# Three more convolution taps on VectorE, later waits ahead of the down products, and ten side tiles per feed-forward block moved to its down chunks

## The chip, the cores and the metric

The kernel runs on one core of a Trainium2 chip. The metric is the device time of one execution in microseconds (us), as the median over runs. The kernel writes its instructions for each engine by hand: TensorE (PE) multiplies, VectorE (DVE) adds and scales, ScalarE (ACT) applies activations and copies, GpSimd (POOL) and SyncE (SP) mostly issue transfers (DMA).

## The reference

Four layers in two blocks work on 256 tokens of width 1024, in float32 (the first layer also has 256 context tokens). Each layer is: half a feed-forward block (FFN), a mixer, another half FFN. A modulation vector per layer, the product of a 1024-wide condition with a 1024 x 9216 matrix, shifts, scales and gates each of them.

```python
def swiglu(y, w_gu, w_down):
    gate, up = jnp.split(y @ w_gu, 2, axis=-1)          # 1024 -> 2 x 2816
    return (jax.nn.silu(gate) * up) @ w_down            # 2816 -> 1024

def half_ffn(h, m, off, g, w_gu, w_down):
    y = modulate(h, g, m[off], m[off + 1])
    return h + 0.5 * m[off + 2] * swiglu(y, w_gu, w_down)

def odd_mixer(y, w_in, conv_w, conv_b, cnorm_g, pool_w, pool_scale, w_out):
    z = y @ w_in
    ga, gb, q = jnp.split(z, [D_CONV, 2 * D_CONV], axis=-1)      # D_CONV = 768
    u = ga * jax.nn.sigmoid(gb)
    u = conv_general_dilated(u, conv_w, ...) + conv_b            # depthwise, 31 taps
    u = jax.nn.silu(rmsnorm(u, cnorm_g))
    ...
    return jnp.concatenate([u, p], axis=-1) @ w_out
```

The other mixers (a recurrent one, a gated linear attention, a latent attention) are not touched.

## The kernel before

**The eight FFNs.** They are F[0] to F[7] in the order of their run. F[0] works on 512 tokens (`wide_one`), the others on 256. Each runs 15 chunks: 11 gate chunks (`u` = 0 to 10, each 256 of the 2816 gate columns and the same of the up columns, 2 MB of weights), then 4 down chunks (`d` = 0 to 3, each 256 of the 1024 outputs, 2.8 MB of weights). A chunk is a matrix product of 2 x 2 blocks done in seven products after Strassen and Winograd. Product `p` takes a sum of weight blocks and a sum of token blocks (table `PRODUCT`) and goes to a PSUM bank pair (BX, BY, BQ, BZ, BW). PE does them in the order 1, 4, 2, 6, 7, 5, 3. In a gate chunk a product is 8 matmuls, in a down chunk 11, one for each "unit tile" `k` of 256 hidden columns, which gate chunk `k` made. The trace has two records for one of these float32 matmuls.

**What DVE does beside it.** The weight sums S1 (L2739), S2 (L2744), S3 (L2748) and S4 (L2753); the sums of token blocks of each unit tile, T1, T2, T4 and T3 (L2762 to L2769, called by `hidden_sums`); and the additions that read the products. In a down chunk these are: the addition of BX to X (L2860), then the sum that empties BY (L2870), then S4, the sum with BZ (L2875), and more. Product 5 writes to BY, so it waits until L2870 has read product 6. The last thing on DVE in a chunk but one is S1 of the next chunk, which waits for that chunk's weights.

**The waits at the first down chunk.** T4 of the last unit tile is made after the last gate chunk's last product has been read, activated and multiplied (L2826, L2827, an activation on ACT, L2830, then T1, T2, T4). Product 4 reads T4 of all 11 unit tiles, and waits for the last of them ahead of its first matmul.

**Weights.** SP loads them into two slots (W0, W1) in turn. The load for a chunk is issued when the chunk two before it has ended (`free`), as two transfers. So the weights of down chunk `d` travel while chunk `d`-1 runs.

**Row tiles.** The modulation vectors of layers 0 to 3 are mostly made on DVE: a row tile (128 x 1024 of the matrix, 512 KB) is multiplied by the condition and summed along its rows in one instruction (L2692, function `ada`). 36 tiles are done in each of F[1] to F[6], none in F[7]. The list `some` says how many per chunk. Tiles lie in a ring of 8 buffers (ADAW). POOL issues the load of a tile as soon as the tile 8 before it has been used (L2406), so a tile used is at once a tile loaded. In a gate chunk the tiles come after S3; in a down chunk all but one come after S3, ahead of the addition of BX to X, and the last one after L2860's third call.

**The convolution** is in layer 1, between F[2] and F[3]. Its 768 channels are 6 stages `f` of 128. Of its 31 taps the first `VTAPS` are done on DVE, as one multiply-add (L1454) each over 128 x 256, two stages side by side; the other `PTAPS` are matmuls on PE with a diagonal matrix that ACT makes (L1407, L1389). When both are done, DVE adds the two parts (L1460), and the squares, their sum on PE and the norm follow.

```python
for f in range(CT_):                    # PE
    pe.wait_ge(s_dg, f + 1)
    pe.wait_ge(s_cu, f + 1)
    for k in range(PTAPS):
        last = mm(PS[CBANK[f]][:, 0:S], DIAG[:, f % 3, k], UP[:, f, VTAPS + k:VTAPS + k + S], ...)
```

Of the kernel before, what the change touches and what calls it, by code (L numbers as in the profile page):

```python
# [19 lines left out]
PAIRS = FT // 2  # L20
# [148 lines left out]
def build(nc, t, out, table_at, stop=None):  # L169

    stop = STOP if stop is None else stop
    with ExitStack() as ctx:
# [200 lines left out]
        def block_bank(b, q, half):  # L373
            at = half * q if b[0] == b[1] else 0
            return PS[b[q]][:, at:at + half]
# [21 lines left out]
        s_th = sem("hidden_sums_ready")  # L397
        s_wh = sem("wide_hidden_sums_ready")
        s_fa = sem("small_ffn_scalar_step")
        s_fd = sem("small_ffn_vector_step")  # L400
# [927 lines left out]
        QM = region(6016, [2, S])  # L1328
        POOLM = region(6528, [4, 2, S])
        SQC = region(8704, [CT_, S])  # L1330
        VTAPS = 20
        PAD = CW // 2
        CBANK = (0, 1, 2, 3, 4, 6)
        PTAPS = CW - VTAPS
        DIAG = region(10240, [3, PTAPS, P])
# [859 lines left out]

        mixers = {}

        some = [0] + [2] * 10 + [4] * 4
        F = [block_ffn(f1[0], d1[0], [2, 4, 4, 4, 4, 4, 5, 7, 7, 7, 8] + [0] * 4, 0, 2, 0.5, 2 * S)]
        mixers["rwkv"] = rwkv_plan()  # L2200
        F += [block_ffn(f2[0], d2[0], some, 0, 8, 0.5),
# [225 lines left out]
        def _(pe):  # L2427
# [11 lines left out]
            def ffn(sec, n_y):  # L2439
                t0, td, n0, fa0, fd0, i = [sec[name] for name in ("t0", "td", "n0", "fa0", "fd0", "i")]  # L2440
                wide_one = sec["T"] > S
# [54 lines left out]
                def down_waits(d, p):  # L2496
                    n_ = n0 + PAIRS + d
                    fa, fd = fa0 + 3 * PAIRS + d, fd0 + 5 * PAIRS + 6 * d
                    if p == 1:
                        pe.wait_ge(s_fd, fd - 5 if d else fd - 2)  # L2500
                    elif p == 2:
                        pe.wait_ge(s_fa, fa + 1)
                    elif p == 3:
                        pe.wait_ge(s_s4, n_ + 1)
                        pe.wait_ge(s_ev, td + 7 * d)
                    elif p == 4:
                        if d:
                            pe.wait_ge(s_fd, fd - 2)
                        elif wide_one:
                            pe.wait_ge(s_wh, 3)  # L2510
                        else:
                            pe.wait_ge(s_th, 4 * PAIRS * i - 1)
                    elif p == 5:
                        pe.wait_ge(s_fd, fd + 2)
                    elif p == 6:
                        pe.wait_ge(s_s2, n_ + 1)
                        pe.wait_ge(s_fd, fd - 1)
                    elif p == 7:
                        pe.wait_ge(s_s3, n_ + 1)
                        if d:  # L2520
                            pe.wait_ge(s_fd, fd)
                        elif wide_one:
                            pe.wait_ge(s_wh, 4)
                        else:
                            pe.wait_ge(s_th, 4 * PAIRS * i)

                for d in range(4):
                    c = sec["w0"] + PAIRS + d
                    w = down_blocks(sec, PAIRS + d)
                    pe.wait_ge(s_w[c % 2], 32 * (c // 2 + 1))  # L2530
                    for p in order_of(sec, PAIRS + d):
                        left, right, b = PRODUCT[p]
                        down_waits(d, p)
                        for k in range(PAIRS):
                            last = mm(block_bank(b, 0, half), w[left][:, k], hb[right][:, k],  # L2535
                                      start=(k == 0 and p not in (2, 5)), stop=(k == PAIRS - 1),
                                      skip_group_check=p in (2, 5))
                        last.then_inc(s_mm, 1)
# [486 lines left out]
```

## Time and profile before

| | |
|---|---|
| median of 3 runs | 3040.9 us (3039.69 to 3043.85) |
| the profiled execution's own time | 3042.03 us |
| its span in the trace | 3040.2 us |
| PE busy | 2874.1 us (95%) |
| DVE busy | 2041.0 us (67%) |
| DMA engines, mean rate | 169 GB/s |

The span runs from the first to the last instruction of the profile, and the execution's own time is 1.8 us more. Times in the timelines count from the start of the span. A release in brackets behind a row, "[1.26 <-DVE ARENA L2768]", says how long the engine sat idle before this row, and what ended it.

### The profile page before, as it was taken

The page shows a single profiled execution, that of the slowest core. Times are in us where ns is not written, and L with a number is a line of the kernel's source. Part 1 is how long each engine was busy: PE and PEld are TensorE (multiplying, and loading weights), DVE is VectorE, ACT ScalarE, POOL GpSimd, SP SyncE. Part 2 cuts the span into 40 slices and gives each one's busy share as a digit, 9 for nine tenths or more (in the row PEclk, how much of TensorE's full clock was granted, in tenths as well). Part 3 has the DMA queues.
Part 4 walks back from the last instruction along what each step waited for, and adds up shares of the span by engine and source line. Part 5 has one row for each costly group of instructions (what it writes and reads, how often), then busy time and mean ns, then how long its engine had stood idle before and what let it go on. Part 6 is the DMA issues. An engine that isn't in the chain of part 4 may idle for free.

```text
span 3040.2 us, 62638 instructions
## 1 busy us (share of the span) xinstructions
PE 2874.1 (95%) x27464; PEld 2658.5 (87%) x27464; DVE 2041.0 (67%) x3534; ACT 568.9 (19%) x1283; POOL 306.4 (10%) x518
## 2 busy tenths in 40 slices
PE   7999998889888999999999999989999999998998
PEld 6888886777887999998889999977889989977998
DVE  6777537545664887885668878826258878853664
ACT  2000004343332101002210021024111021032101
POOL 0001002422430000000000100000000100000000
PEclk8999999999999999999999999999999999999999
DMA  7557313013005686786257867643367857823452
GB/s 277 166 184 244 109 45 108 4 45 98 18 4 181 213 272 222 243 265 213 70 191 253 284 199 255 219 119 111 127 213 254 283 177 251 263 73 97 139 187 91
DMA packets 387503, 514.53 MB, mean 169 GB/s; under 512 B 14032, under 2 KB 344976, under 8 KB 386080
## 3 DMA queue, kind: packets, MB, share of 16 engines
q1 hardware_dynamic: 347632, 366.73, 37.3%
q0 software_dynamic: 39456, 143.67, 13.8%
q8 instruction: 217, 3.56, 0.5%
q14 instruction: 54, 0.44, 0.0%
q10 hardware_dynamic: 144, 0.13, 0.0%
HBM read 509.44 MB, written 1.05 MB: 168 GB/s over the span
## 4 chain that ended last, share of the span: by engine, by line
PE 86%; DVE 5%; DMA 4%; ACT 3%; issue 2%; POOL 1%; SPq 0%; DVEq 0%; ACTq 0%; POOLq 0%
PE PS L2491 39%; PE PS L2535 19%; PE PS L630 6%; PE PS L650 5%; PE PS L807 3%; PE PS L1706 2%; PE PS L2547 2%; PE PS L1631 2%; DMA W<-in_ffn_out 1%; DMA W<-in_ffn_w_down 1%; PE PS L1389 1%; PE PS L2435 1%; PE PS L1483 1%; PE PS L2568 1%; PE PS L666 1%
## 5 line engine op out<-in xcount | busy, mean ns | idle before, releaser
L2491 PE MATMUL PS<-Y,W 128*128 128x128 f32 (+1 forms) x5456 | 713.2, 289 | 36.3 <-ACT Y L2628 30.5
L2491 PEld LDWEIGHTS PS<-Y,W 128*128 128x128 f32 x5456 | 677.9, 195 | 55.4 <-issue 35.0
L2491 PE MATMUL PS<-Y,ARENA 128*128 128x128 f32 (+1 forms) x3872 | 477.7, 280 | 0.0
L2491 PEld LDWEIGHTS PS<-Y,ARENA 128*128 128x128 f32 x3872 | 458.5, 192 | 4.5
L2535 PE MATMUL PS<-ARENA,W 128*128 128x128 f32 (+1 forms) x2816 | 364.2, 288 | 10.8 <-DVE ARENA L2768 7.9
L2535 PEld LDWEIGHTS PS<-ARENA,W 128*128 128x128 f32 x2816 | 346.9, 192 | 22.3 <-DVE ARENA L2768 9.7
L2406 POOL DMA_DIRECT2D ADAW<-in_ada_rows x272 | 144.4, 532 | 1873.1 <-DVE ADAW L2692 1527.7
L2692 DVE SCALAR_TENSOR_TENSOR ADAW<-ADAW,CB 128x1024 f32<-128x1024 f32 x280 | 332.0, 1219 | 0.2
L2739 DVE TENSOR_TENSOR ARENA<-W 128x1024 f32<-128x1024 f32 (+1 forms) x120 | 159.3, 1327 | 12.9 <-DMA W<-in_ffn_out 4.9
L2748 DVE TENSOR_TENSOR W<-W 128x1024 f32<-128x1024 f32 (+1 forms) x120 | 158.9, 1324 | 0.0
L2744 DVE TENSOR_TENSOR ARENA<-ARENA,W 128x1024 f32<-128x1024 f32 (+1 forms) x116 | 152.5, 1314 | 0.3
L2535 PE MATMUL PS<-ARENA 128*128 128x128 f32 x1232 | 146.7, 275 | 0.0
L630 PE MATMUL PS<-Y,W 128*128 128x256 f32 (+2 forms) x560 | 128.0, 392 | 15.0 <-ACT Y L2628 13.1
L2535 PEld LDWEIGHTS PS<-ARENA 128*128 128x128 f32 x1232 | 142.1, 192 | 0.0
L650 PE MATMUL PS<-W 64*64 64x64 f32 x4608 | 114.2, 223 | 27.3 <-issue 24.0
L630 PEld LDWEIGHTS PS<-Y,W 128*128 128x128 f32 (+2 forms) x560 | 107.7, 193 | 35.2 <-issue 14.9
L2600 ACT ACTIVATE SIL<-SIL 128x256 f32<-128x256 f32 x77 | 32.1, 417 | 565.5 <-DVE SIL L2826 565.5
L650 PEld LDWEIGHTS PS<-W 64*64 64x64 f32 x4608 | 100.3, 136 | 38.9 <-issue 35.0
L807 PE MATMUL PS<-Y,W 128*128 128x256 f32 x528 | 123.6, 394 | 10.7 <-ACT Y L2628 4.6
L807 PEld LDWEIGHTS PS<-Y,W 128*128 128x128 f32 x528 | 102.5, 197 | 31.5 <-issue 13.4
L2753 DVE TENSOR_TENSOR ARENA<-W,ARENA 128x1024 f32<-128x1024 f32 x88 | 107.2, 1218 | 0.0
L1317 DVE SCALAR_TENSOR_TENSOR X<-PS,HG,X 128x256 f32<-128x256 f32 x32 | 15.5, 484 | 125.0 <-PE PS L630 50.9
(425 smaller groups left out, 3736.3 us busy)
## 6 DMA issues: line engine op xcount, KB each, us to landing
ADAW<-in_ada_rows POOLq DMA_DIRECT2D x272, 512.0 KB, 4.7
W<-in_ffn_w_gu SPq DMA_DIRECT2D x88, 1024.0 KB, 7.6
W<-in_ffn_in SPq DMA_DIRECT2D x88, 1024.0 KB, 7.4
W<-in_ffn_w_down SPq DMA_DIRECT2D x32, 1408.0 KB, 9.3
W<-in_ffn_out SPq DMA_DIRECT2D x32, 1408.0 KB, 9.2
W<-in_even_w_in SPq DMA_DIRECT2D x40, 512.0 KB, 4.6
W<-in_e_w_in SPq DMA_DIRECT2D x16, 512.0 KB, 4.9
W<-in_e_w_in SPq DMA_DIRECT2D x8, 1024.0 KB, 7.5
```

Of the source, the lines that this page charges most:

```text
L630: last = mm(PS[idx % 4][0:m_, 0:S], wide(c, kt, n_)[:, k, q * P:q * P + m_], x(k), start=(k == 0), stop=(k == kt - 1))
L650: last = mm(to, x, y, start=(k == 0), stop=(k == len(pairs) - 1))
L807: last_ = mm(PS[at[f] % 4][:, 0:S], w[:, k, q * P:(q + 1) * P], Y[:, k, off:off + S], start=(k == 0), stop=(k == DT - 1))
L1631: last = mm(PS[idx % 4][:, 0:S], wide(c, DT)[:, k, (i % 2) * P:(i % 2 + 1) * P], Y[:, k, 0:S], start=(k == 0), stop=(k == DT - 1))
L2406: pool.dma_start(ADAW[:, g % 2, i], t["ada_rows"][g * P:(g + 1) * P, i * D:(i + 1) * D])\
L2491: last = mm(block_bank(b, q, half), w[left][:, k, q * P:(q + 1) * P], yb[right][:, k], start=(k == 0 and p not in (2, 5)), stop=(k == 3), ...
L2535: last = mm(block_bank(b, 0, half), w[left][:, k], hb[right][:, k], start=(k == 0 and p not in (2, 5)), stop=(k == PAIRS - 1), skip_group_ ...
L2692: V.scalar_tensor_tensor(w, w, 1.0, CB[:, 0 if layer < 2 else 1], ALU.mult, ALU.mult, accum_out=MOD[:, layer, tile + i:tile + i + 1]).then ...
L2739: V.tensor_tensor(w["S1"], w["A21"], w["A22"], ALU.add).then_inc(s_s1, 1)
L2744: V.tensor_tensor(w["S2"], w["S1"], w["A11"], ALU.subtract).then_inc(s_s2, 1)
L2748: V.tensor_tensor(w["S3"], w["A11"], w["A21"], ALU.subtract).then_inc(s_s3, 1)
L2753: V.tensor_tensor(w["S4"], w["A12"], w["S2"], ALU.subtract).then_inc(s_s4, 1)
```

## The change

It does three things. `VTAPS` goes from 20 to 23, so `PTAPS` from 11 to 8. The list `some` goes from 2 row tiles in each of the gate chunks 1 to 10 and 4 in each down chunk to 1 in each gate chunk and 6, 6, 7, 7 in the down chunks; the sum stays 36. And in down chunk 0 of F[1] to F[7], PE waits ahead of products 1 and 4 only for what unit tile 9 and the banks need, and for unit tile 10 ahead of the last matmul of the product.

```diff
-        VTAPS = 20
+        VTAPS = 23
...
-        some = [0] + [2] * 10 + [4] * 4
+        some = [0] + [1] * 10 + [6, 6, 7, 7]
...
                     if p == 1:
-                        pe.wait_ge(s_fd, fd - 5 if d else fd - 2)
+                        if d:
+                            pe.wait_ge(s_fd, fd - 5)
+                        else:
+                            pe.wait_ge(s_fa, fa - 1)
+                            pe.wait_ge(s_fd, fd - 7)
...
                         elif wide_one:
                             pe.wait_ge(s_wh, 3)
                         else:
-                            pe.wait_ge(s_th, 4 * PAIRS * i - 1)
+                            pe.wait_ge(s_fd, fd - 2)
+                            pe.wait_ge(s_th, 4 * (PAIRS * i - 1))
...
                         for k in range(PAIRS):
+                            if d == 0 and k == PAIRS - 1:
+                                if p == 1:
+                                    pe.wait_ge(s_fd, fd0 + 5 * PAIRS - 2)
+                                elif p == 4 and not wide_one:
+                                    pe.wait_ge(s_th, 4 * PAIRS * i - 1)
                             last = mm(block_bank(b, 0, half), w[left][:, k], hb[right][:, k], ...)
```

The lines after the first added one move down: PE's matmul of the down chunks is L2535 before and L2545 after, and DVE's lines from L2692 on are 10 higher.

PE at the start of down chunk 0 of F[1], products 1, 4 and 2, before (hidden_sums_ready counts T1 to T4, small_ffn_vector_step counts DVE's additions and multiplications):

```order
L2535 MATMUL PS<-ARENA,W 128x128 [waits small_ffn_vector_step,weights_loaded1]
L2535 MATMUL PS<-ARENA,W 128x128 x10
L2535 MATMUL PS<-ARENA,W 128x128 [waits hidden_sums_ready]
L2535 MATMUL PS<-ARENA,W 128x128 x10
L2535 MATMUL PS<-ARENA,W 128x128 [waits small_ffn_scalar_step]
```

The same place after the change:

```order
L2545 MATMUL PS<-ARENA,W 128x128 [waits small_ffn_vector_step,small_ffn_scalar_step,weights_loaded1]
L2545 MATMUL PS<-ARENA,W 128x128 x9
L2545 MATMUL PS<-ARENA,W 128x128 [waits small_ffn_vector_step]
L2545 MATMUL PS<-ARENA,W 128x128 [waits hidden_sums_ready,small_ffn_vector_step]
L2545 MATMUL PS<-ARENA,W 128x128 x9
L2545 MATMUL PS<-ARENA,W 128x128 [waits hidden_sums_ready]
L2545 MATMUL PS<-ARENA,W 128x128 [waits small_ffn_scalar_step]
```

Each of the two products has a wait of its own ahead of its eleventh matmul now.

DVE in down chunk 1 of F[1], from S3 to S4, before (modulation_rows_loaded0 to 7 are the buffers of the ring):

```order
L2748 TENSOR_TENSOR W<-W 128x11x128
L2692 SCALAR_TENSOR_TENSOR ADAW,MOD<-ADAW,CB 128x1024 [waits modulation_rows_loaded0]
L2692 SCALAR_TENSOR_TENSOR ADAW,MOD<-ADAW,CB 128x1024 [waits modulation_rows_loaded1]
L2692 SCALAR_TENSOR_TENSOR ADAW,MOD<-ADAW,CB 128x1024 [waits modulation_rows_loaded2]
L2860 SCALAR_TENSOR_TENSOR X<-PS,HG,X 128x128 [waits dense_tile_done]
L2870 TENSOR_TENSOR SIL<-JUNK,PS 128x128 [waits dense_tile_done,small_ffn_scalar_step]
L2753 TENSOR_TENSOR X<-W,ARENA 128x1408 [waits weight_sum2_ready]
```

After the change:

```order
L2758 TENSOR_TENSOR W<-W 128x11x128
L2702 SCALAR_TENSOR_TENSOR ADAW,MOD<-ADAW,CB 128x1024 [waits modulation_rows_loaded0]
L2702 SCALAR_TENSOR_TENSOR ADAW,MOD<-ADAW,CB 128x1024 [waits modulation_rows_loaded1]
L2702 SCALAR_TENSOR_TENSOR ADAW,MOD<-ADAW,CB 128x1024 [waits modulation_rows_loaded2]
L2702 SCALAR_TENSOR_TENSOR ADAW,MOD<-ADAW,CB 128x1024 [waits modulation_rows_loaded3]
L2702 SCALAR_TENSOR_TENSOR ADAW,MOD<-ADAW,CB 128x1024 [waits modulation_rows_loaded4]
L2870 SCALAR_TENSOR_TENSOR X<-PS,HG,X 128x128 [waits dense_tile_done]
L2880 TENSOR_TENSOR SIL<-JUNK,PS 128x128 [waits dense_tile_done,small_ffn_scalar_step]
L2763 TENSOR_TENSOR X<-W,ARENA 128x1408 [waits weight_sum2_ready]
```

Five tiles instead of three stand ahead of the addition of BX and the sum that empties BY (L2880 now).

## Rows read from the trace of the kernel before

**Rows 1.** The page: span, PE and DVE busy (us, share, instructions)

```profile
span 3040.2 us, 62638 instructions
PE 2874.1 (95%) x27464; PEld 2658.5 (87%) x27464; DVE 2041.0 (67%) x3534; ACT 568.9 (19%) x1283; POOL 306.4 (10%) x518
```

**Rows 2.** Timeline of PE in the convolution (start, length)

```profile
1474.78 5.02 PE L1389 MATMUL PS<-ARENA 128*128 128x256 f32 x22
1479.72 2.00 PE L1397 MATMUL PS<-ARENA 128*64 128x256 f32 x16
1481.65 24.02 PE L1389 MATMUL PS<-ARENA 128*128 128x256 f32 x110
```

**Rows 3.** Timeline of DVE in the convolution

```profile
1473.30 15.13 DVE L1454 SCALAR_TENSOR_TENSOR ARENA<-ARENA,VEC 128x256 f32<-128x256 f32 x38
1488.53 0.75 DVE L1460 TENSOR_TENSOR ARENA<-ARENA,PS 128x256 f32<-128x256 f32 x2
...
1505.71 0.42 DVE L1460 TENSOR_TENSOR ARENA<-ARENA,PS 128x256 f32<-128x256 f32 x1 [4.33 <-PE PS L1389]
```

**Rows 4.** Groups by line and shape: busy, mean ns, idle before, its releasers

```profile
L2535 PE MATMUL PS<-ARENA,W 128*128 128x128 f32 x2464 | 286.4, 275 | 8.7 <-DVE ARENA L2768 6.3 <-DMA W<-in_ffn_out 1.8 <-DMA W<-in_ffn_w_down 0.5
L2739 DVE TENSOR_TENSOR ARENA<-W 128x1408 f32<-128x1408 f32 x32 | 52.0, 1625 | 9.5 <-DMA W<-in_ffn_out 4.9 <-DMA W<-in_ffn_w_down 3.9
```

**Rows 5.** Timeline of PE, start of down chunk 0 of F[2]

```profile
1343.83 2.62 PE L2535 MATMUL PS<-ARENA,W 128*128 128x128 f32 x22
1347.71 5.18 PE L2535 MATMUL PS<-ARENA,W 128*128 128x128 f32 x44 [1.26 <-DVE ARENA L2768]
```

**Rows 6.** Timeline of DVE, same place

```profile
1343.37 1.62 DVE L2739 TENSOR_TENSOR ARENA<-W 128x1408 f32<-128x1408 f32 x1 [0.70 <-DMA W<-in_ffn_w_down]
...
1347.37 0.29 DVE L2768 TENSOR_TENSOR ARENA<-ARENA 128x128 f32<-128x128 f32 x1
...
1350.85 1.22 DVE L2692 SCALAR_TENSOR_TENSOR ADAW<-ADAW,CB 128x1024 f32<-128x1024 f32 x1
...
1354.29 0.34 DVE L2860 SCALAR_TENSOR_TENSOR X<-PS,HG,X 128x128 f32<-128x128 f32 x1
1355.46 0.29 DVE L2870 TENSOR_TENSOR SIL<-JUNK,PS 128x128 f32<-128x128 f32 x1 [0.83 <-PE PS L2535]
```

**Rows 7.** Timeline of PE, start of down chunk 0 of F[6]

```profile
2609.06 2.72 PE L2535 MATMUL PS<-ARENA,W 128*128 128x128 f32 x22 [1.76 <-DMA W<-in_ffn_out]
2613.39 5.18 PE L2535 MATMUL PS<-ARENA,W 128*128 128x128 f32 x44 [1.61 <-DVE ARENA L2768]
```

**Rows 8.** Windows, down chunks 1 and 2 of F[2], then of F[7] (PE, PEld, DVE, ACT, POOL, clock, DMA share, GB/s)

```profile
1362.60:1379.80 17.20, 17.20 (x157) 17.20 (x156) 13.86 (x23) 0.28 (x1) 2.12 (x4) 1.00 0.87 291
1379.80:1397.00 17.20, 17.20 (x157) 17.20 (x156) 13.71 (x23) 0.28 (x1) 2.12 (x4) 1.00 0.87 291
2970.00:2987.20 17.20, 17.20 (x156) 17.20 (x155) 9.38 (x15) 0.28 (x1) 0.00 (x0) 1.00 0.52 170
2987.20:3004.40 17.20, 17.20 (x156) 17.20 (x155) 9.37 (x15) 0.28 (x1) 0.00 (x0) 1.00 0.53 169
```

**Rows 9.** Timeline of PE, starts of down chunks 2 and 3 of F[2]

```profile
1379.75 7.53 PE L2535 MATMUL PS<-ARENA,W 128*128 128x128 f32 x66
...
1396.95 3.29 PE L2535 MATMUL PS<-ARENA,W 128*128 128x128 f32 x28
```

**Rows 10.** Timeline of DVE in down chunks 1 and 2 of F[2]

```profile
1372.65 0.29 DVE L2870 TENSOR_TENSOR SIL<-JUNK,PS 128x128 f32<-128x128 f32 x1 [2.17 <-PE PS L2535]
...
1378.94 1.62 DVE L2739 TENSOR_TENSOR ARENA<-W 128x1408 f32<-128x1408 f32 x1
...
1396.37 1.62 DVE L2739 TENSOR_TENSOR ARENA<-W 128x1408 f32<-128x1408 f32 x1 [0.35 <-DMA W<-in_ffn_w_down]
```

**Rows 11.** Weight load of down chunk 3 by its line: issue, landing; F[2]

```profile
L2359 SPq DMA_DIRECT2D W<-in_ffn_w_down x2: 368/751/1134, 1379.9 to 1380.4; - x2
...
DMA to landing us min/median/max: 8.6/12.3/15.9
```

**Rows 12.** The same load in F[7]

```profile
DMA to landing us min/median/max: 6.3/8.1/9.9
```

## The prediction

> **What bounds the kernel now.** I read the page's first part, then the groups with what ended their idle time, then timelines of PE and DVE at the three places that the change touches, and last the windows and the landing times of the weight loads. PE is busy 2874.1 of 3040.2 us [rows 1], so only what shortens PE's work or removes a wait of PE counts. DVE has a third of the span free, but not everywhere: in a down chunk it is busy 13.86 of 17.20 us [rows 8].
>
> Three places matter. (1) In the convolution PE does its products back to back and DVE waits 4.33 us for each of the last ones [rows 2, 3]. (2) At the step from gate to down chunks of F[1] to F[7], PE's idle time is 8.7 us in all: 6.3 for T4 (L2768) and 2.3 for late weights [rows 4]. (3) In the down chunks PE doesn't wait, but the weights come just in time: in F[2] S1 of chunk 3 waited 0.35 us for them, 0.58 us ahead of the chunk's own start [rows 9, 10].
>
> **Term 1, the taps.** The last five stages of 11 products take 24.02 us [rows 2]; the steps are 4.75 us (DVE's 4.33 of idle and 0.42 of work, [rows 3]), so one product takes 0.432. 3 x 6 = 18 go: 7.8 us. DVE gets 18 more multiply-adds of 15.13/38 = 0.398 us [rows 3], 7.2 us: its taps end at 1488.53 + 7.2 = 1495.7 instead of 1488.5, and after five additions of 0.75/2 it would be at 1497.6. PE ends at 1505.7 - 7.8 = 1497.9 and releases the sixth and last. So DVE's work is covered by PE's with nearly nothing to spare, and the gain is the full 7.8. If a tap cost DVE the full 0.48 of a lone one (no row hints at it), 1.2 us of it would go. I take -7.8. ACT makes 18 diagonals less, which nothing waits for: PE's products run on without a gap there.
>
> **Term 2, the wait for T4.** Product 1 of down chunk 0 starts at 1343.83 in F[2]; a product of 11 matmuls takes 17.20/7 = 2.46 us [rows 9]. Product 4 could start at 1346.29 and starts at 1347.71 [rows 5]. With the wait at the eleventh matmul, T4 is needed 10 x 2.46/11 = 2.2 us later. No wait of F[1] to F[7] exceeds 1.61 [rows 7] where 2.2 are given, so all 6.3 us go there. The same change at product 1 gives nothing: PE waited there for weights alone [rows 4].
>
> But they come back at product 5, which waits for L2870. From the start of T4 (1347.37) to the start of L2870 without its wait are 1355.46 - 0.83 - 1347.37 = 7.3 us [rows 6]; two more row tiles of (1354.29 - 1350.85)/3 = 1.15 each make it 9.6. It would end at 1357.2. PE, no longer stopped, is at product 5 at 1343.83 + 5 x 2.46 = 1356.1. So it stops there for 1.1 us, and of 1.26 only 0.16 is kept. What can help is that T4 itself comes earlier: S1 of the first down chunk waits 0.70 us for its weights, and DVE holds T4 up behind it [rows 6]. The move takes one row tile's load out of the last gate chunks. I price a tile from the windows: (0.87 - 0.52) x 17.20/4 = 1.5 us of all DMA engines [rows 8]. That covers the 0.70 and, in F[6] and F[1], most of the 2.3 us by which PE waited for weights [rows 4, 7]. Bounds: between 0.5 (only F[7], which has no row tiles) and 8.7. I take the middle, -4.4.
>
> **Term 3, ten more tiles in the down chunks.** DVE has the time: it has 3.3 us free in a chunk [rows 8]; two tiles need 2.3, three need 3.4. Of its idle time 2.17 us stand right before L2870 [rows 10], where most of the tiles go, so there it is just used up. I put 0.2 us for each of 12 chunks with more tiles than fit well at a third of them: +0.8.
>
> The transfers are the other half. Each tile used is a tile loaded. With four tiles a chunk the DMA engines are busy 0.87 of the time, without any 0.52 [rows 8]; at 1.5 us a tile, six make 0.87 + 3.0/17.2 = 1.04, and seven 1.13. The weights of the next chunk are in that queue. Their second transfer lands 15.9 us after its issue at 1380.4 with four tiles [rows 11], and 9.9 us after without [rows 12]: again 1.5 us for a tile. PE needs them at 1396.95, S1 at 1396.02, and they land at 1396.3 [rows 9 to 11]: 0.7 us of margin. The upper bound is the whole delay: two tiles, 3.0 us, less 0.9 of margin at chunk 2 (S1 there ran at 1378.94 and PE at 1379.75), and three tiles, 4.5 less 0.7 at chunk 3, less the 2.1 by which the chunk is late already: 3.8 for an FFN, 23 for six. The lower bound is nothing. What speaks for less than the bound: in chunk 1 the tiles come some 1.1 us later against the weights, since DVE is later; the tiles at the end of a burst may land in the next chunk; and all 32 S1 of this size waited 8.8 us for weights [rows 4], 0.3 on average, so other FFNs have more margin than F[2]. I take a third: +7.
>
> **The sum.** -7.8 - 4.4 + 7.8 = -4.4 us on the profiled execution, which took 3042.0 us, 1.1 above the median. On the median: 3040.9 - 4.4 = 3036.5; I say 3036.
>
> The Trainium skill (DMA: Bandwidth & Descriptors, section "Queues, rings and completion order") says that each DMA engine goes round the queue rows that have work and drains a whole packet of descriptors from one before it turns to the next. By that rule a row tile that is queued is not held back by the weights, so each of them delays their last bytes as long as any are left. The 1.5 us for each of four tiles agrees with it [rows 11, 12]. By the rule term 3 would be at its upper bound, which is the second rival.
>
> **The rivals.** *Hidden loads:* the additional tiles travel in the time that the DMA engines have left, and the weights are not later. For it: a share of 0.87 leaves 2.2 us, and the longer bursts may end in the next chunk's start, where the weights are only issued. Against it: 1.04 and 1.13 are more than there is. Then term 3 is 0 to 1, and the sum -12: 3029. *Late weights in full:* the row tiles' bursts are served before the last of the weights, at 1.5 us each. Term 3 is then +23.8, the sum +11.6: 3053. It is one mechanism, and decides as soon as the weights of chunks 2 and 3 come late by 11.4/6 = 1.9 us for an FFN: there the gain of terms 1 and 2 is gone. *Taps only, the rest a draw:* delays of 8 to 16 us eat term 2 and most of term 1, sum -4 to +4 around 3041; it differs from my forecast in size alone. *The waits do nothing:* PE stops at product 5 for as long as it did at product 4. That is inside term 2's bound.
>
> **How the numbers follow.** A measurement here tells changes of over 0.2%, 6.1 us, from none. Forecast (sum -9 to 0): 0.45, of which 0.14 lie beyond -6.1. Hidden loads (-10 to -16): 0.26. The draw (0 to +6): 0.15. Late weights in full (over +6): 0.14. So faster 0.40, same 0.46, slower 0.14. The forecast's own range is 3032 to 3041. The range for 8 in 10 takes most of the hidden loads and of the late weights: 3027 to 3049.
>
> **What would show it.** In the convolution: L1389 with x16 records for a stage, 3.45 us apart, and the last L1460 at 7.8 us less from the first; if it waits for no PE, DVE has become the bound. At down chunk 0: no idle time of PE for L2768 (L2778 now); idle time of about 1 us ahead of product 5 for L2880 would show the stall moved. In the down chunks: DMA share near 1.0 where it was 0.87, and idle time of PE ahead of chunks 2 and 3 for W. No such idle time is the first rival, over 2 us for an FFN the second. The prediction is most likely wrong in term 3, which I could only bound.

## The result, and the profile after

The changed kernel took 3053.25 us in the median of 5 runs (3051.6 to 3063.3); the kernel before took 3041.34 in the median of its 5. The ratio is 1.0043, with a 95% interval of 1.0024 to 1.0062: slower by 0.4% (the ratio is estimated from all the runs and is not the quotient of the two medians, 1.0039). The prediction was 3036, with a range of 3027 to 3049: the time lies outside the range, and the change went the other way. The time measured is that of the second rival, late weights in full (3053).

The profiled execution took 3053.18 us. Its page: span and busy times, and the shares of the engines in the chain that ended last. Before, DMA had 4% of that chain and PE 86%.

```profile
span 3051.4 us, 62573 instructions
PE 2872.0 (94%) x27428; PEld 2657.4 (87%) x27428; DVE 2043.1 (67%) x3552; ACT 563.2 (18%) x1265; POOL 306.6 (10%) x518
PE 81%; DMA 7%; DVE 5%; ACT 3%; issue 2%; POOL 1%; SPq 0%; DVEq 0%; ACTq 0%; POOLq 0%
```

PE has 18 products of the convolution less, 7.8 us, and yet it is busy only 2.1 us less than in [rows 1]. The groups by line and shape say why:

```profile
L2545 PE MATMUL PS<-ARENA,W 128*128 128x128 f32 x2464 | 294.6, 281 | 18.6 <-DMA W<-in_ffn_w_down 9.8 <-DMA W<-in_ffn_out 8.7
L2545 PE MATMUL PS<-ARENA 128*128 128x128 f32 x1232 | 147.2, 275 | 1.9 <-DVE SIL L2880 1.9
L2749 DVE TENSOR_TENSOR ARENA<-W 128x1408 f32<-128x1408 f32 x32 | 52.0, 1624 | 29.5 <-DMA W<-in_ffn_w_down 15.2 <-DMA W<-in_ffn_out 13.6
```

Against [rows 4]: the T4 wait (6.3 us) is gone from the first row, and 18.5 us of waits for weights stand in its place, where there were 2.3. The same 2464 records take 294.6 us instead of 286.4. DVE's S1 (L2749 now) waits 28.8 us for weights instead of 8.8.

**Where PE waits** for weights is one place in each of F[1] to F[6]: ahead of down chunk 2 (0.5 us more come at chunk 0 of F[1]). Timeline of PE in F[2], from down chunk 0 to 2:

```profile
1347.00 7.53 PE L2545 MATMUL PS<-ARENA,W 128*128 128x128 f32 x66
...
1359.93 2.72 PE L2545 MATMUL PS<-ARENA 128*128 128x128 f32 x22 [0.48 <-DVE SIL L2880]
...
1364.94 7.53 PE L2545 MATMUL PS<-ARENA,W 128*128 128x128 f32 x66
...
1384.36 9.26 PE L2545 MATMUL PS<-ARENA,W 128*128 128x128 f32 x66 [2.05 <-DMA W<-in_ffn_w_down]
```

The first row answers to [rows 5]: products 1, 4 and 2 now run without a stop. The second is the stall at product 5 that the prediction had worked out; it is 0.48 us where 1.1 were expected. The last row is the loss. PE waits 2.05 us for weights, and then the same three products take 9.26 us instead of 7.53. Windows of F[2] show what the second part is: the idle stretch, the start of chunk 2 and its rest (columns as in [rows 8]).

```profile
1382.20:1384.30 2.10, 0.10 (x1) 0.00 (x0) 0.00 (x0) 0.00 (x0) 0.00 (x0) 1.00 0.71 268
1384.40:1387.40 3.00, 3.00 (x16) 3.00 (x17) 3.00 (x3) 0.00 (x0) 0.00 (x0) 0.58 0.98 326
1388.50:1403.20 14.70, 14.70 (x134) 14.70 (x134) 13.93 (x26) 0.28 (x1) 3.71 (x7) 1.00 0.96 324
```

After the wait the granted clock is 0.58 for 3 us, so mostly the lower of its two levels, 1.2 GHz, and PE does 16 records in them; from 1388.5 on it is 1.00, 2.4 GHz, with 27 records in 3 us (134 in 14.7). From the starts of chunks 2 and 3 in the timelines, chunk 2 takes 18.9 us in F[1] to F[6] (18.7 in F[5]) instead of 17.2. That is 10.1 us in all, in slower records and not in waits. The first row of the groups agrees, if it is set against the version without any such wait further down (294.6 - 284.5 = 10.1); before, that row had 286.4 us, 1.9 more than a version without T4's waits.

**The weights.** The load of down chunk 2 in F[2] by its line:

```profile
L2359 SPq DMA_DIRECT2D W<-in_ffn_w_down x2: 367/944/1522, 1365.1 to 1365.5; - x2
...
DMA to landing us min/median/max: 8.8/13.8/18.8
```

Before, this load took 15.7 us; now 18.8, and 20.9 in F[1] instead of 16.1. Chunk 3's, on which the prediction counted for nearly half of its bound, delays nothing. In F[2] it is issued by 1382.7, when chunk 1 has ended, and lands 14.5 us later, at 1397.2; chunk 3 starts at 1403.3, because chunk 2 itself started late and ran 1.7 us longer.

**The convolution** went as predicted. PE, then DVE:

```profile
1480.25 3.72 PE L1389 MATMUL PS<-ARENA 128*128 128x256 f32 x16
...
1485.83 17.54 PE L1389 MATMUL PS<-ARENA 128*128 128x256 f32 x80
```

```profile
1501.13 1.75 DVE L1460 TENSOR_TENSOR ARENA<-ARENA,PS 128x256 f32<-128x256 f32 x5
1503.41 0.42 DVE L1460 TENSOR_TENSOR ARENA<-ARENA,PS 128x256 f32<-128x256 f32 x1 [0.54 <-PE PS L1389]
```

PE's last five stages take 17.54 us instead of 24.02, and the first takes 3.72 instead of 5.02: 7.8 less. DVE still waits for PE at the last addition, 0.54 us, where the prediction had 0.3.

**The ledger.** The stretches between the starts of chunks, as PE's timeline has them, after minus before, summed over the FFNs:

| stretch | us |
|---|---|
| from the end of F[2] to F[3], with the convolution | -8.6 |
| from the last gate chunk to down chunk 1, F[1] to F[7] | -7.3 |
| down chunk 1 with the wait behind it, F[1] to F[6] | +19.1 |
| down chunk 2, F[1] to F[6] | +10.1 |
| all else (the head alone -3.4) | -2.2 |
| sum | +11.1 |

Stretches that the change does not touch differ by up to 6 us between two executions (the one between F[0] and F[1] was 0.4 longer here, 6.2 longer in rows_only below), so below only the stretches that a question is about are compared.

### The profile page after: what moved, and what is told of

The parts are those of the page before. It is cut to its first block, busy times and chain, and to the rows that moved or that the text cites. A ratio compares the mean times of both kernels' runs of the same rounds, so it can differ in the third digit from the quotient of the medians.

```text
span 3051.4 us, 62573 instructions
## 1 busy us (share of the span) xinstructions
PE 2872.0 (94%) x27428; PEld 2657.4 (87%) x27428; DVE 2043.1 (67%) x3552; ACT 563.2 (18%) x1265; POOL 306.6 (10%) x518
## 4 chain that ended last, share of the span: by engine, by line
PE 81%; DMA 7%; DVE 5%; ACT 3%; issue 2%; POOL 1%; SPq 0%; DVEq 0%; ACTq 0%; POOLq 0%
PE PS L2491 39%; PE PS L2545 15%; PE PS L630 6%; PE PS L650 5%; PE PS L807 3%; DMA W<-in_ffn_w_down 3%; DMA W<-in_ffn_out 3%; PE PS L1706 2%; PE PS L2557 2%; PE PS L1631 2%; PE PS L2435 1%; PE PS L1483 1%; DVE ADAW L2702 1%; PE PS L1389 1%; PE PS L2578 1%
## 5 line engine op out<-in xcount | busy, mean ns | idle before, releaser
L2545 PE MATMUL PS<-ARENA,W 128*128 128x128 f32 (+1 forms) x2816 | 372.4, 293 | 20.6 <-DMA W<-in_ffn_w_down 9.8
L2545 PEld LDWEIGHTS PS<-ARENA,W 128*128 128x128 f32 x2816 | 355.9, 196 | 31.7 <-DMA W<-in_ffn_w_down 10.6
L2749 DVE TENSOR_TENSOR ARENA<-W 128x1024 f32<-128x1024 f32 (+1 forms) x120 | 159.3, 1328 | 33.1 <-DMA W<-in_ffn_w_down 15.2
L2545 PE MATMUL PS<-ARENA 128*128 128x128 f32 x1232 | 147.2, 275 | 1.9 <-DVE SIL L2880 1.9
L2545 PEld LDWEIGHTS PS<-ARENA 128*128 128x128 f32 x1232 | 142.0, 192 | 2.7 <-DVE SIL L2880 2.7
L630 PE MATMUL PS<-Y,W 128*128 128x256 f32 (+2 forms) x560 | 128.0, 392 | 14.8 <-ACT Y L2638 13.1
L2817 DVE TENSOR_TENSOR SIL<-JUNK,PS 128x256 f32<-128x256 f32 x77 | 32.5, 422 | 115.5 <-PE PS L2491 115.5
```

The costliest lines, as they stand in the source:

```text
L630: last = mm(PS[idx % 4][0:m_, 0:S], wide(c, kt, n_)[:, k, q * P:q * P + m_], x(k), start=(k == 0), stop=(k == kt - 1))
L2749: V.tensor_tensor(w["S1"], w["A21"], w["A22"], ALU.add).then_inc(s_s1, 1)
```

## The experiments

All were timed beside the kernel before on the same chip; that one's median moved between 3041 and 3048 from chip to chip, so the ratio is what to compare. Under tiles, the first number is for the ten gate chunks together; "waits" says whether the later waits are in (new) or not (old).

| run | tiles: gate; down | taps | waits | median us (runs) | ratio, 95% interval |
|---|---|---|---|---|---|
| changed kernel | 10; 6 6 7 7 | 23 | new | 3053.25 (5) | 1.0043, 1.0024 to 1.0062 |
| rows_back | 20; 4 4 4 4 | 23 | new | 3024.3 (4) | 0.993, 0.9913 to 0.9947 |
| rows_only | 10; 6 6 7 7 | 20 | old | 3069.13 (4) | 1.0072, 1.005 to 1.0095 |
| small_loads | 10; 6 6 7 7, 1/16 of the bytes | 23 | new | 3026.0 (4) | 0.9934, 0.9913 to 0.9955 |
| fill | 10; 6 6 7 7 | 23 | new | 3055.19 (7) | 1.0037, 1.0023 to 1.0052 |
| edges | 15; 6 4 4 7 | 23 | new | 3024.77 (4) | 0.9944, 0.9922 to 0.9965 |
| middle | 15; 4 6 7 4 | 23 | new | 3019.23 (4) | 0.9931, 0.9908 to 0.9953 |
| all_five | 16; 5 5 5 5 | 23 | new | 3026.13 (8) | 0.9954, 0.9937 to 0.997 |
| first_two | 15; 6 6 4 5 | 23 | new | 3055.76 (10) | 1.0036, 1.002 to 1.0051 |
| seven_in_one | 15; 4 7 6 4 | 23 | new | 3037.83 (10) | 0.9978, 0.9964 to 0.9991 |
| taps_only | 20; 4 4 4 4 | 23 | old | 3028.69 (10) | 0.9961, 0.9949 to 0.9972 |
| waits_only | 20; 4 4 4 4 | 20 | new | 3037.31 (10) | 0.9974, 0.9961 to 0.9988 |
| taps_24 | 20; 4 4 4 4 | 24 | new | 3028.24 (5) | 0.9944, 0.9924 to 0.9963 |

### Which part is to blame: rows_back and rows_only

rows_back is the changed kernel with the old list, rows_only the kernel before with the new list:

```diff
-        some = [0] + [1] * 10 + [6, 6, 7, 7]
+        some = [0] + [2] * 10 + [4] * 4
```

> The changed kernel with the old list of row tiles (2 in each gate chunk, 4 in each down chunk); the 23 taps and the later waits stay. Theory (the row tiles' loads make the weights of down chunk 2 late, and PE's clock is low after that wait): no wait for weights at chunk 2, chunks 2 of 17.2 us, the taps' 7.8 and the 6.3 us of waits for T4 are gained: 3041.3 - 14 = 3027 us. Rival (the later waits let PE run ahead of the weights, so they share the blame): waits for weights at chunk 2 stay in part, over 3035 us.

> The kernel before with the new list of row tiles alone; 20 taps, old waits. Theory: the waits of the changed kernel at down chunk 2 (19.1 us in all) and the slow chunks behind them (10.1 us) come back whole, against some 3 us less for late weights at down chunk 0: 3041 + 26 = 3067 us. Rival (blame shared with the later waits): less than +15 us, under 3056.

rows_back: 3024.3, faster than before by 0.7%. rows_only: 3069.13, slower by 0.7%. Both are near what was expected, and both rivals, by which the later waits share the blame (over 3035 and under 3056), fall. The groups of rows_back, then of rows_only:

```profile
L2545 PE MATMUL PS<-ARENA,W 128*128 128x128 f32 x2464 | 284.5, 275 | 0.1
L2545 PE MATMUL PS<-ARENA 128*128 128x128 f32 x1232 | 146.7, 275 | 0.0
```

```profile
L2535 PE MATMUL PS<-ARENA,W 128*128 128x128 f32 x2464 | 292.8, 279 | 27.6 <-DMA W<-in_ffn_w_down 11.0 <-DMA W<-in_ffn_out 10.2 <-DVE ARENA L2768 6.2
```

With the old list 0.1 us of waits are left and no record is slower, and with the new list alone 21.2 us of waits for weights, beside T4's old 6.2. So the move of the row tiles alone makes the loss, and the other two parts gain. In rows_only chunks 1 and 2 of F[1] to F[6] are 27.0 us longer than before, in the changed kernel 29.2.

The same rows settle two smaller points of the prediction. PE's idle time at product 5 is nothing with three tiles ahead of L2880 in chunk 0, and 1.9 us with the five of the changed kernel: it takes the moved tiles to make that stall, as the prediction had worked out. And the relief that one tile fewer in the gate chunks was to give T4 doesn't show: the waits for T4 are 6.2 us in rows_only and were 6.3 before. The step from gate to down chunks, read as in the ledger, is 10.7 us shorter in rows_back and only 7.3 in the changed kernel.

### The transfers or DVE's work: small_loads

The tiles that POOL loads for F[1] to F[6], but for the first eight of F[1] and of F[5], bring 64 of their 1024 columns; DVE's work stays in its place. So this kernel leaves out most of the matrix behind the modulation rows, and scales what DVE makes of it by 0.25.

```diff
-                pool.dma_start(ADAW[:, g % 2, i], t["ada_rows"][g * P:(g + 1) * P, i * D:(i + 1) * D])\
+                cut = D // 16 if all(not 0 <= n - F[i]["row0"] < RING for i in (1, 5)) and n >= F[1]["row0"] else D
+                pool.dma_start(ADAW[:, g % 2, i, 0:cut], t["ada_rows"][g * P:(g + 1) * P, i * D:i * D + cut])\
...
-                V.scalar_tensor_tensor(w, w, 1.0, CB[:, 0 if layer < 2 else 1], ALU.mult, ALU.mult,
+                V.scalar_tensor_tensor(w, w, 1.0 if n < F[1]['row0'] else 0.25, CB[:, 0 if layer < 2 else 1], ALU.mult, ALU.mult,
```

> The changed kernel, whose row tiles of F[1] to F[6] load 64 of 1024 columns (but for the first 8 tiles after each of two pauses), and scale by 0.25, so the modulation vectors are not the reference's; DVE does as many instructions of the same size at the same places. Theory (loads): no wait for weights at down chunk 2, all chunks at 17.2 us, about 3024 to 3028 us. Rival (DVE is too full with 5 or 6 tiles ahead of L2880): stays at 3045 to 3053 us, with PE waiting for DVE.

3026.0. S1 of the down chunks in this run:

```profile
L2750 DVE TENSOR_TENSOR ARENA<-W 128x1408 f32<-128x1408 f32 x32 | 52.0, 1624 | 3.4 <-DMA W<-in_ffn_out 1.3 <-DMA W<-in_ffn_w_down 1.3
```

These are 2.6 us of waits for weights instead of 28.8, with the same instructions on DVE. PE waits for no weights at all ahead of a down chunk, and chunks 1 and 2 take 17.2 us each. The bytes of the tiles are the cause, and not DVE's time. The kernel ran 1.7 us above rows_back, less than the spread of either.

### What the clock costs: fill

```diff
+                    if d == 2 and 1 <= i <= 6:
+                        for _ in range(12):
+                            mm(NORM_PS[:, 0:P], ones, ident, start=True, stop=True)
```

Twelve products that nobody reads, ahead of PE's wait at down chunk 2.

> The changed kernel with 12 idle matmuls of 128x128 (2.7 us) on PE ahead of down chunk 2 of F[1] to F[6], into a bank that nothing reads then; the results are not used. They fit into the wait for weights of 2.2 to 4.4 us in most of the six. Theory (PE's clock falls because PE stood still for over 2 us): chunk 2 takes 17.2 instead of 18.9 us, some 8 to 10 us less in all: 3043 to 3046 us. Rival (the slow chunk has another cause, such as the matmuls' own waits or the memory): chunk 2 stays at 18.9 and the time at 3053 or above.

Expected 3043 to 3046, measured 3055.19: a miss. In the profile the clock did what was expected of it. Groups of fill (the line is L2548 there):

```profile
L2548 PE MATMUL PS<-ARENA,W 128*128 128x128 f32 x2464 | 285.2, 275 | 4.5 <-DMA W<-in_ffn_w_down 3.5 <-DMA W<-in_ffn_out 0.9
L2548 PE MATMUL PS<-ARENA 128*128 128x128 f32 x1232 | 147.9, 276 | 4.5 <-DVE SIL L2883 4.5
```

The records are back at 275 ns, and chunk 2 takes 17.4 to 17.8 us, so the rival by which it stays at 18.9 is refuted, although the time that it named, 3053 or above, came. Beside the filler (2.84 us in F[1]), 4.4 us of waits for weights are left. Chunks 1 and 2 together are 23.1 us longer than before instead of 29.2: what chunk 2 is longer went from 10.1 us to 2.3, and what chunk 1 is longer, with the filler and the wait, from 19.1 to 20.9. Product 5 now waits 4.5 us for DVE instead of 1.9, and the step to chunk 1 lost 2.7 us against the changed kernel. So the stretches that the filler can reach are some 3 us shorter than in the changed kernel, and the 8 to 10 us expected were too much. The ratios of the two, 1.0037 and 1.0043, can't tell 3 us from none.

The profiled execution, 3061.86 us, was 6.7 above the median of the run. Three stretches that nothing edited, the head, F[0] to F[1] and F[4] to F[5], are 3.4, 2.5 and 6.4 us longer in it than in the profile of the changed kernel. What the slower clock costs in time is therefore read from the records alone and not shown by a run. The waits themselves are not in doubt.

### Which tiles: edges, middle, all_five, first_two, seven_in_one

Each is the changed kernel with another list, 36 tiles in all. edges and middle split the change in two. In their order, edges, middle, all_five:

```diff
-        some = [0] + [1] * 10 + [6, 6, 7, 7]
+        some = [0] + [2] * 5 + [1] * 5 + [6, 4, 4, 7]
+        some = [0] + [2] * 5 + [1] * 5 + [4, 6, 7, 4]
+        some = [0] + [2] * 6 + [1] * 4 + [5] * 4
```

> The changed kernel with 6, 4, 4, 7 tiles in the down chunks and 15 in the gate chunks: the extra tiles of chunks 0 and 3 stay, those of chunks 1 and 2 go back. Theory: what costs is a tile loaded while the weights of chunk 2 travel, that is in chunk 1; the weights of chunk 1 have slack and those of chunk 3 too. Then no wait for weights ahead of chunk 2, chunks 1 and 2 take 17.2 us each, and the time is 3024 to 3028. Rival: the two extra tiles of chunk 0 are loaded late, still in the queues in chunk 1, and push the weights of chunk 2 as well; then chunk 2 waits 1 to 3 us in each of six FFNs and the time is 3033 to 3050.

> The changed kernel with 4, 6, 7, 4 tiles in the down chunks and 15 in the gate chunks: the reverse of the run before. Theory: the whole loss is made in chunk 1; PE waits 2 to 4 us for weights ahead of chunk 2 of F[1] to F[6], chunk 2 takes 18.9 us, and the time is 3050 to 3056. Rival (the extra tiles of chunk 0 share the blame): the waits are half as long, and the time is 3035 to 3045.

> The changed kernel with 5 tiles in each down chunk and 16 in the gate chunks. With 1.5 us of all DMA engines for a tile and a margin of 0.9 us the weights of chunk 2 would be 0.6 us late in each FFN: the time is 3028 to 3032 if PE keeps its clock after so short a wait. Rival: a tile delays them by 2.5 us (half of what two did in F[2]'s chunk 3), then they are 1.6 us late, the clock falls too, and the time is 3036 to 3045.

middle refuted my theory. It has the six tiles in chunk 1 that were to make all of the loss, and ran at 3019.23 where 3050 to 3056 were expected, with no wait for weights but one of 0.5 us. edges has four there and ran at 3024.77, as expected and also without loss. Each half of the change is free; only both together cost. So the rival that went with middle, half of the waits, fell as well. Chunk 2's weights in F[2], first in edges, then in middle:

```profile
L2359 SPq DMA_DIRECT2D W<-in_ffn_w_down x2: 368/1074/1780, 1359.4 to 1359.8; - x2
...
DMA to landing us min/median/max: 9.5/13.2/16.9
```

```profile
L2359 SPq DMA_DIRECT2D W<-in_ffn_w_down x2: 368/658/949, 1356.5 to 1356.9; - x2
...
DMA to landing us min/median/max: 6.8/10.5/14.1
```

PE needs the weights 16.8 us after the issue (in F[2] of the changed kernel they landed after 18.8, and PE waited 2.05). Over F[1] to F[6] they landed after 16.1 to 16.9 us in edges, which leaves it no margin, and after 13.9 to 16.2 in middle; the kernel before had 13.9 to 16.1. In all_five they landed after 17.1 to 18.5 us in four FFNs, and after 15.0 and 15.9 in F[4] and F[5], so neither price of a tile, 1.5 or 2.5 us, holds. PE waited 4.3 us ahead of chunk 2 in all six together. None of these waits, 1.8 us at the most, was followed by a slower chunk, and the time was 3026.13, below both ranges. The landing is not a sum of tiles, then: in F[2], 4 and 6 tiles give 14.1 us, 5 and 5 give 18.5.

Two more lists, first_two and seven_in_one, asked whether the two chunks' tiles have to come together.

```diff
+        some = [0] + [2] * 5 + [1] * 5 + [6, 6, 4, 5]
+        some = [0] + [2] * 5 + [1] * 5 + [4, 7, 6, 4]
```

> The changed kernel with 6, 6, 4, 5 tiles in the down chunks and 15 in the gate chunks. Six tiles in chunk 0 alone cost nothing, nor six in chunk 1 alone, so the theory now is that it takes both: three tiles left over from chunk 0 when chunk 2's weights are issued, so that some DMA engines lag, and a burst of five tiles in chunk 1, which these engines carry ahead of or between the last weights. Then PE waits for weights ahead of chunk 2 as in the changed kernel, 2 to 4 us in each of six FFNs, chunk 2 takes 18.9 us, and the time is 3048 to 3054. Rival: what counts is the total over the four chunks (26 in the changed kernel, 21 here and in the two runs that lost nothing); then there is no wait and the time is 3019 to 3026.

> The changed kernel with 4, 7, 6, 4 tiles in the down chunks and 15 in the gate chunks. Theory: with one tile left over when chunk 2's weights are issued no DMA engine lags far enough to be caught by the burst, however long it is; these weights land 14 to 16 us after their issue as with six tiles, and PE does not wait for them. Chunk 3's do come with two or more tiles left over and a burst of five, and land later, 17 us or more. DVE has 0.1 us too little time in chunk 1. Time 3020 to 3030. Rival: each tile in a burst adds its 1.5 us, only the base is lower; then chunk 2's weights land 17 us or more after issue and the time is 3028 to 3040.

first_two: 3055.76, a little above the expected 3048 to 3054, though 21 tiles lie in the down chunks as in middle and edges. Its group is the changed kernel's over again:

```profile
L2545 PE MATMUL PS<-ARENA,W 128*128 128x128 f32 x2464 | 294.5, 281 | 17.1 <-DMA W<-in_ffn_w_down 9.8 <-DMA W<-in_ffn_out 7.3
```

That rules out the total over the four chunks, and shows that the tiles of chunks 2 and 3 had no part in the loss. seven_in_one came out between: 3037.83, where 3020 to 3030 were expected. That is in the rival's range, 3028 to 3040. Its landings for chunk 2 run from 14.8 us (F[6]) to 19.4 (F[1]), so a burst of six tiles ahead of L2880 can catch the last weights even with little left over from chunk 0. My "however long it is" is refuted, and the rival's "each tile adds its 1.5 us" fits as little: in F[6] they landed after 14.8 us with seven tiles, where the kernel before has 15.8 with four. Both factors count: how much is left over, and how long the burst is.

What the DMA queues did in F[2] of the changed kernel shows how. q1 carries the weights (2816 packets a chunk), q0 the row tiles; the columns are packets, MB and share of the 16 engines' time. The stretches are 1366 to 1371 us, 1371 to 1375.5, 1375.5 to 1380 and 1380 to 1384.3; the weights were issued at 1365.1 and landed at 1384.3.

```profile
q1 hardware_dynamic: 1292, 1.32, 76.6%
q0 software_dynamic: 110, 0.38, 19.5%
...
q1 hardware_dynamic: 1433, 1.45, 98.3%
...
q0 software_dynamic: 465, 1.72, 96.2%
q1 hardware_dynamic: 95, 0.10, 6.2%
...
q0 software_dynamic: 345, 1.22, 77.8%
q1 hardware_dynamic: 89, 0.09, 6.9%
```

In the first 5 us a fifth of the engines' time still goes to tiles left over from chunk 0. 10 us after the issue nearly all of the weights have passed (1292 and 1433 packets). The rest, fewer than 200 (of the 89 in the last stretch some are already chunk 3's, issued from 1382.3 on), needs 9 us more, beside the burst of five tiles, which takes 96% of all engines' time in the third stretch. In middle the first 5 us have the weights alone:

```profile
q1 hardware_dynamic: 1532, 1.55, 97.6%
```

and the last weights land at 1371.0, 14.1 us after their issue. My reading is that some engines lag behind the others because of the leftover tiles, and are then caught by the burst. The completion marks in the traces support it; each of the two transfers of a load has 16. Of the second transfer in F[2] of the changed kernel, 12 marks have come 10.3 us after its issue, and the other four come after 13.4, 14.2, 16.3 and 18.8. The first transfer is through before the burst's bytes flow; its last mark comes 8.4 us after that issue here, and after 6.4 in middle. So the lag is there ahead of the burst, and longer with leftover tiles. No run changed the order inside an engine by itself, so the last step of this reading stays an inference.

The Trainium skill (DMA: Bandwidth & Descriptors, section "Queues, rings and completion order") has the rule that each engine goes round the queues with work, packet by packet; these rows do not contradict it, and do not show the order either. The prediction had taken from it that each tile delays the last weights by its own time, and middle shows that this is not so.

### The two parts that gain: taps_only, waits_only, taps_24

taps_only is the kernel before with one number changed, waits_only has the three places of the waits, and taps_24 is rows_back with one number changed:

```diff
-        VTAPS = 23
+        VTAPS = 24
```

> The kernel before with 23 taps and nothing else. Theory: 18 products of 0.432 us go from PE and DVE's taps stay covered: 7.8 us less, 3034 to 3037. Rival: the rest of the gain of the version with the old row tiles was more than the waits' 10 us, and the taps give only 2 to 4, as DVE has 0.3 us of margin.

> The kernel before with the later waits of products 1 and 4 and nothing else. The traces of the versions with the waits show 10.5 to 10.7 us less from the last gate chunk to chunk 1, that with the taps alone 4.5 less, so the waits are worth 6: 3034 to 3037. Rival: their gain comes back at product 5 in full, as the prediction had it for F[2]; 3038 to 3042.

> The version with the taps and waits of the change and the row tiles of before, with 24 taps on DVE instead of 23. PE has 6 products of 0.43 us less, but DVE, which with 23 taps waited only 0.54 us for the last one, does 6 multiply-adds of 0.40 more: 2.4 us. The last addition (L1460) then waits for nothing, the section from F[2] to F[3] is 1.8 us longer than with 23 taps, and the time is 3025 to 3028 (that version ran at 3024.3). Rival: DVE's additions of the first five stages are hidden elsewhere, the section is no longer and the time the same or 1 us less.

taps_only: 3028.69, below the expected 3034 to 3037 and not where the rival had it. The ratio is 0.9961, 11.9 us with an interval of 8.5 to 15.5; the section from F[2] to F[3] is 8.6 us shorter in its profile, 7.8 of it in the convolution. The theory of 7.8 us holds for the convolution; the gain in the time is larger than what the edit explains. The step into the down chunks of F[6], with the two waits of [rows 7], is 3.2 us shorter here too, though nothing of it was edited; that may be part of it. waits_only: 3037.31 and a ratio of 0.9974, so 7.9 us with an interval of 3.6 to 11.9, where 6 were expected: the theory holds, and the rival, all given back at product 5, falls. (Its range, 3038 to 3042, is near the time, but this run's kernel before took 3045.43. The prediction had the gain come back only with two more tiles ahead of L2880; this run has no moved tiles.) The groups of waits_only have no idle time for T4 and none for product 5:

```profile
L2545 PE MATMUL PS<-ARENA,W 128*128 128x128 f32 x2464 | 284.4, 275 | 0.8 <-DMA W<-in_ffn_w_down 0.8
L2545 PE MATMUL PS<-ARENA 128*128 128x128 f32 x1232 | 146.7, 275 | 0.0
```

taps_24: 3028.24, and a ratio of 0.9944 against 0.993 of rows_back. The intervals overlap, so the time alone doesn't say that it is worse; its profile does. DVE, and behind it PE:

```profile
1498.33 2.07 DVE L1460 TENSOR_TENSOR ARENA<-ARENA,PS 128x256 f32<-128x256 f32 x6
```

```profile
1480.24 15.38 PE L1389 MATMUL PS<-ARENA 128*128 128x256 f32 x70
1499.89 5.41 PE L2557 MATMUL PS<-ARENA,CT 128*128 128x256 f32 x12 [4.28 <-ACT ARENA L2621]
```

DVE does all six additions without a wait, so it is the bound. PE stands idle for 4.28 us before the sum of squares, and then takes 5.41 us for 12 records that take 2.75 in rows_back, at a granted clock of 0.51. The window of that stretch, and one behind the next wait of PE:

```profile
1499.80:1505.20 5.40, 5.30 (x13) 4.28 (x14) 0.61 (x2) 2.52 (x3) 0.00 (x0) 0.51 0.00 0
1509.40:1513.40 4.00, 4.00 (x10) 3.19 (x11) 0.20 (x1) 1.53 (x4) 0.00 (x0) 0.50 0.00 0
```

PE reaches the sum of squares 1.8 us later after the start of the convolution than in rows_back, just as expected. But the sum then costs 2.7 us more, and the 124 records of L1483 behind it 2.9 more (29.96 us instead of 27.03). They follow a wait of 3.22 us, which rows_back has as well, at a granted clock of 1.00 behind it. So the section from F[2] to F[3] is 6.2 us longer than in rows_back where I had expected 1.8: the wait for DVE was foreseen, and the clock behind it forgotten, as in the prediction.

## Why the prediction was wrong

**Term 1, the taps: right.** -7.8 predicted, -7.8 in the timelines of the convolution. The margin on DVE was called nearly nothing, and one tap more uses it up.

**Term 2, the waits: right in mechanism, too low in size.** -4.4 predicted, -7.3 at the boundary of the changed kernel, of which 3.5 lie in F[6], where the taps alone bring 3.2. The stall did move to product 5, and the moved tiles made it, as worked out: 1.9 us in four FFNs (0.9 at most), where 1.1 was forecast for F[2] (0.48 there). The help from the tile less in the last gate chunks was wrong: T4's waits are 6.2 us in rows_only as against 6.3. Alone, the waits give 7.9 us (3.6 to 11.9).

**Term 3, the moved tiles: this step failed.** The words were "I take a third: +7". It measured 29.2: 19.1 of waits and 10.1 of slower records behind them. The other part of the term, 0.8 us for DVE's time in chunks 1 to 3, did not show: in small_loads, with all its tiles on DVE, none of them is longer than before. Three parts of the +7 were off.

- *The size.* The failed step is the third. In F[2] the full bound for chunk 2 was 2.1 us and the wait was 2.05, but the bound was then divided by three because other FFNs had more margin. They had: chunk 2's weights landed after 13.9 to 16.1 us before. In the changed kernel they landed after 18.8 to 20.9, 3.1 us later in F[2] and 4.8 in F[1], and F[2], taken as the tightest, had the shortest wait of the six. That the bound fitted F[2] was luck: the price of 1.5 us for a tile came from a mean share and from single loads of F[2] and F[7] [rows 8, 11, 12], while chunk 3's load took 11.4 us in F[6] of the same trace, also with four tiles, and middle shows that the tiles don't add up.
- *The place.* The bound was made of 2.1 us at chunk 2 and 1.7 at chunk 3. All of it came at chunk 2, 2 to 4 us in each FFN, and nothing at chunk 3. That a late chunk 2 gives the load of chunk 3 its time back I had allowed for, but with 2.1 us instead of 2 to 4 and the slower chunk behind it.
- *What was missing.* PE's clock. The waits of 2 to 4 us ahead of chunk 2 were followed by a chunk 1.5 to 1.7 us longer. The profile of before had nothing of the kind in its down chunks (behind the 1.26 us of [rows 5] the granted clock was 1.00), and the prediction has no term for it. By the ledger the changed kernel would be slower by 1 us even without it, 11.1 less 10.1; fill could not show that in the time.

**The rivals.** Late weights in full had the right time, 3053, and the right condition: it was to decide from 1.9 us for an FFN, and the loss at chunk 1 and its wait is 3.2 on average. It had the sum partly by luck, since its 23.8 us stand for 29.2, with 2.9 us more than forecast from term 2, 0.8 more from the section with the convolution and 2.2 from elsewhere against them. Its chance, 0.14, was too low. Its mechanism, each tile delays the last weights by its own time, is refuted by middle. Hidden loads is wrong for this list and right for middle and edges.

## What to carry to other kernels

When transfers move to another place, count what is still in the queues when the next urgent load is issued and what comes while its last bytes travel; a mean share of the DMA engines hides both, and either alone may be free. A short wait of PE can have a second price, the clock behind it, so a term for late data needs it too. When a change has parts, time the parts: here two of them were worth 0.7% (rows_back, or middle, which has the same ratio within the intervals), and the third ate it and more.

## What the runs showed of the hardware

The last bytes of a load can be far behind the rest: in F[2] of the changed kernel, all but at most 200 of some 2800 packets had passed after 10 us, and these took 9 more beside a burst of row tiles. The delay is not linear in the number of tiles. In F[2], 4 and 6 tiles in two chunks landed after 14.1 us, 5 and 5 after 18.5, 6 and 4 after 16.9, 6 and 6 after 18.8. With one list the six FFNs differ by up to 4.6 us (14.8 to 19.4 in seven_in_one).

PE's clock falls after short waits, but not after all of them. With waits up to 1.8 us (all_five) PE did chunk 2 in at most 17.3 us. With 2.0 us (F[2] of the changed kernel) it took 18.9, and with 2.90 in F[2] of rows_only 17.4. In F[3] of seven_in_one a wait of 1.89 us ahead of chunk 3 was enough: this chunk took 19.1 us instead of 17.4. The length of the wait alone doesn't decide. In first_two PE waited 2.48 us ahead of chunk 2 both in F[4] and in F[6]; here are the rows behind these waits, with a window for each:

```profile
1947.79 7.63 PE L2545 MATMUL PS<-ARENA,W 128*128 128x128 f32 x66 [2.48 <-DMA W<-in_ffn_out]
...
2654.81 9.26 PE L2545 MATMUL PS<-ARENA,W 128*128 128x128 f32 x66 [2.48 <-DMA W<-in_ffn_out]
```

```profile
1947.90:1950.90 3.00, 3.00 (x27) 3.00 (x28) 3.00 (x3) 0.28 (x1) 0.00 (x0) 1.00 1.04 354
2654.90:2657.90 3.00, 3.00 (x19) 3.00 (x20) 3.00 (x3) 0.00 (x0) 0.00 (x0) 0.66 1.07 367
```

The granted clock is 1.00 behind the first wait and 0.66 behind the second, and chunk 2 takes 17.3 and 18.9 us. What makes the difference is open. Behind the waits of fill, 1.5 us at most after its filler products, chunk 2 took 17.4 to 17.8 us. In taps_24 a wait of 4.28 us was followed by a granted clock of 0.51.
